# Attention block of a hybrid decoder step: loads two steps ahead, LRU stores not waited for at the block's end, and a turned copy between ScalarE's two exponents

## The reference

```
z = h @ w_in                      # columns: q | k | v | LRU branch | LRU gate
for each of 4 heads, two softmaxes c = 0, 1 over 64-wide halves of q and k:
    s_c = q_c k_c^T / 8 - slope_h * (i - j), causal
    p   = softmax(s_0) - lam * softmax(s_1)
    o   = p @ v                   # 128 wide; RMSNorm, gain g_subln, times (1 - lam_init)
RG-LRU: conv of width 4, gates, linear scan, times gelu(gate branch)
mix = concat(o, lru) @ w_out ;  then the SwiGLU FFN
```

## Time and profile before

| | |
|---|---|
| median of the runs | 3118.41 us |
| the profiled execution, its time | 3117.97 us |
| its span | 3115.9 us |
| PE busy | 2699.2 us (87%) |
| DVE busy | 1691.1 us (54%) |
| ACT busy | 1051.4 us (34%) |
| POOL busy | 912.3 us (29%) |
| chain that ended last | PE 45% of the span, DVE 3%, DMA 2% |

### The profile page before, as it was taken

One profiled execution on the slowest core, in us unless ns is written; L12 is line 12 of the kernel. 1 busy time (PEld: TensorE's weight loads), 2 busy tenths in 40 slices (PEclk: granted clock), 3 DMA queues, 4 the chain that ended last, 5 costly groups with the idle time before them and its releaser, 6 DMA issues.

```text
span 3115.9 us, 42980 instructions
## 1 busy us (share of the span) xinstructions
PE 2699.2 (87%) x16348; PEld 2536.9 (81%) x16348; DVE 1691.1 (54%) x2477; ACT 1051.4 (34%) x1608; POOL 912.3 (29%) x399
## 2 busy tenths in 40 slices
PE   5999998488888656874499999999978999999994
PEld 2999998467777516774499999999978999999993
DVE  2689776567677451667344444444475444444446
ACT  3545553267777503444211111111231111111111
POOL 2566655222332105443122222212241122222212
PEclk8999999699999868987699999999999999999997
DMA  5345433333332255545411111111133111111122
GB/s 217 119 145 190 155 127 128 96 95 82 106 92 65 69 198 194 204 156 176 160 62 41 40 43 58 40 40 61 40 116 90 61 40 40 58 43 40 40 74 55
DMA packets 164737, 300.53 MB, mean 96 GB/s; under 512 B 15402, under 2 KB 131274, under 8 KB 158482
## 3 DMA queue, kind: packets, MB, share of 16 engines
q1 hardware_dynamic: 154850, 283.56, 27.6%
q10 hardware_dynamic: 9776, 15.46, 1.5%
HBM read 252.63 MB, written 46.39 MB: 96 GB/s over the span
## 4 chain that ended last, share of the span: by engine, by line
PE 45%; DVE 3%; DMA 2%; ACT 1%; POOL 0%; issue 0%; DVEq 0%; ACTq 0%; POOLq 0%
PE p_y L1918 15%; PE p_g L1902 15%; PE p_u L1902 15%; DMA p_stage<-h 1%; DVE p_y L2100 1%; DVE p_xin L2112 1%; DVE p_h_lo L2089 1%; ACT p_h_hi L2006 0%; DVE p_rstd L2097 0%; POOL p_stage L1862 0%; DVE p_f_lo L2071 0%; DVE p_y L2083 0%; DMA yT<-p_xin 0%; DMA p_xin<-x 0%; ACT p_stage L2015 0%
## 5 line engine op out<-in xcount | busy, mean ns | idle before, releaser
L2083 DVE TENSOR_TENSOR p_y<-p_y 128x342 f32<-128x342 f32 (+1 forms) x1008 | 483.8, 512 | 730.5 <-PE p_y L1918 730.4
L1902 PE MATMUL p_g<-p_h_hi,p_w_hi 128*128 128x342 f32 (+1 forms) x1056 | 341.7, 324 | 31.5 <-DVE p_h_lo L2089 31.5
L1918 PE MATMUL p_y<-p_f_hi,p_w_hi 128*128 128x342 f32 (+1 forms) x1056 | 344.5, 326 | 26.4 <-DVE p_y L2081 14.2
L329 POOL TENSOR_TENSOR p_w_lo<-p_wraw,p_w_hi 128x1024 fp32r<-128x1024 f32 x100 | 294.5, 2955 | 213.9 <-ACT p_w_hi L390 213.7
L1855 POOL TENSOR_TENSOR p_w_lo<-ffn_wraw,p_w_hi 128x1024 fp32r<-128x1024 f32 x66 | 160.8, 2437 | 639.4 <-ACT p_w_hi L1983 639.4
L1918 PE MATMUL p_y<-p_f_hi,p_w_lo 128*128 128x342 f32 (+1 forms) x1056 | 342.0, 324 | 0.0
L1918 PE MATMUL p_y<-p_f_lo,p_w_hi 128*128 128x342 f32 (+1 forms) x1056 | 341.3, 323 | 0.0
L1902 PE MATMUL p_g<-p_h_lo,p_w_hi 128*128 128x342 f32 (+1 forms) x1056 | 340.3, 322 | 0.0
L1902 PE MATMUL p_g<-p_h_hi,p_w_lo 128*128 128x342 f32 (+1 forms) x1056 | 339.4, 321 | 0.0
L1902 PE MATMUL p_u<-p_h_lo,p_w_hi 128*128 128x342 f32 (+1 forms) x1056 | 338.2, 320 | 0.0
L1902 PE MATMUL p_u<-p_h_hi,p_w_hi 128*128 128x342 f32 (+1 forms) x1056 | 337.4, 319 | 0.0
(11 more groups left out here) (257 smaller groups left out, 5809.5 us busy)
## 6 DMA issues: line engine op xcount, KB each, us to landing
p_wraw<-w_in SPq DMA_DIRECT2D x100, 512.0 KB, 4.7
ffn_wraw<-w_ffn SPq DMA_DIRECT2D x22, 1536.0 KB, 6.5
p_wraw<-w_ffn SPq DMA_DIRECT2D x22, 1536.0 KB, 6.5
p_wraw<-w_out SPq DMA_DIRECT2D x48, 512.0 KB, 7.0
p_ada<-w_ada SPq DMA_DIRECT2D x64, 256.0 KB, 3.2
z<-p_zout SPq DMA_DIRECT2D x48, 206.0 KB, 2.9
p_ada_ring<-w_ada SPq DMA_DIRECT2D x4, 2048.0 KB, 20.9
p_qraw<-z SPq DMA_DIRECT2D x64, 128.0 KB, 3.1
```

Of the source, the lines that this page charges most:

```text
L329: pool.tensor_tensor(w_lo[s][:], wraw[:, s, :], w_hi[s][:].bitcast(F32), ALU.subtract).then_inc(lo_done, 1)
L1902: mm = pe.matmul(bk[par][:, 0:W], a[s][:, KT * half + k, :], b[:, k, c0:c0 + W], start=r == 0, stop=r == 3 * KT - 1)
L1918: mm = pe.matmul(yb[q % YB][:, 0:W], a[s][:, 2 * KT + m, :], b[:, c0:c0 + W], start=r == 0, stop=r == 2)
L2083: dve.tensor_tensor(y[:, m, c0:c0 + W], y[:, m, c0:c0 + W], yb[q % YB][:, 0:W], ALU.add).then_inc(yadd, 1)
```

## The change

- `y_out` outlives `input_projection`: the wait at the block's end goes, and `attention` waits for these stores before the first `read_o` on ScalarE and at step 1 on VectorE; `sample_attention` waits once more at its end.
- Start of attention: q unit 0 is loaded by two DMAs that ScalarE issues; SP starts with k units 0 and 1. ScalarE does the high parts of q 0, k 0, k 1 first, q 1 after. On POOL the low part of q 0 comes before the affine select. The scaling of `gsub` moves into VectorE's step 3, and ScalarE waits for it at step 16.
- Loads of k, q, v are issued in iteration s for step s + 2; `load_ada` keeps its iteration but comes behind them, and is one DMA of 512 KB into one buffer. Output stores keep their iteration.
- In each step ScalarE's order is now exponent 0, `read_v`, turned piece 0, exponent 1, turned piece 1, `read_o`. Before it was exponent 0, exponent 1, `read_v`, pieces 0 and 1, `read_o`.

```diff
@@ input_projection, SP
             sp.dma_start(io["conv_kept"], io["state_conv"][:, 1:3, :]).then_inc(y_out, 16)
-            sp.wait_ge(y_out, 16 * (NG + 3))
             for s in range(RW):
                 sp.wait_ge(z_out[s], 16 * (1 + NG * ZC))
@@ attention, POOL
-            pool.wait_ge(S["ready"], 2)
-            pool.affine_select(out=bias[:], in_=bias[:], compare_op=ALU.is_ge, fill=MASKED, base=SEQ - QB,
...
+            q_low(0)
+            pool.wait_ge(S["ready"], 2)
+            pool.affine_select(out=bias[:], in_=bias[:], compare_op=ALU.is_ge, fill=MASKED, base=SEQ - QB,
@@ attention, SP
             def load_ada(i):
-                for half in range(2):
-                    wait(sp, "rows", i)
-                    sp.dma_start(ada[half][:], io["w_ada"][c, :, 4 * half:4 * half + 4, w0:w0 + AW]
-                                 ).then_inc(ada_in[half], 16)
+                wait(sp, "rows", i)
+                sp.dma_start(ada[:], io["w_ada"][c, :, :, w0:w0 + AW]).then_inc(ada_in, 16)
+            def loads(s):
+                for n in range(1, NQ):
+                    if qstep(n) == s:
+                        load_q(n)
+                for h, u in kpreps.get(s, []):
+                    if s > -1:
+                        load_k(h, u)
+                for h, u in vpreps.get(s, []):
+                    load_v(h, u)
+            for x in kpreps[-1]:
+                load_k(*x)
+            loads(-1)
             sp.dma_start(mods["gsub"][:], io["g_subln"].rearrange("o d -> d o")).then_inc(gs_in, 16)
-            load_q(0)
+            loads(0)
+            load_ada(0)
             for s in range(-1, END):
...
+                loads(s + 2)
+                if adas(s + 1):
                     load_ada(adas(s + 1))
+                for t in oturns.get(s - 1, []):
                     store(t)
@@ attention, ACT
+            for part in (slice(0, DH), slice(DH, P)):
+                act.dma_start(qraw[0][part, :, :], halves(0, slice(UQ * UNITS[0][0], UQ * UNITS[0][0] + UQ))
+                              ).then_inc(q_in[0], 16)
...
+                if s == 0:
+                    act.wait_ge(mods["y_out"], 16 * mods["y_stores"])
...
+            q_high(0)
+            for x in kpreps[-1]:
+                k_high(*x)
             for s in range(-1, END):
+                nt = len(turns(s - 2)) if real(s - 2) else 0
                 if real(s - 1):
                     exps(s - 1, 0)
-                    exps(s - 1, 1)
                 for x in vpreps.get(s, []):
                     read_v(x)
-                nt = len(turns(s - 2)) if real(s - 2) else 0
-                for i in range(min(nt, 2)):
-                    copy_turned(s - 2, i)
+                if nt:
+                    copy_turned(s - 2, 0)
+                if real(s - 1):
+                    exps(s - 1, 1)
+                if nt > 1:
+                    copy_turned(s - 2, 1)
                 if real(s - 3):
                     read_o(s - 3)
@@ attention, DVE, in the loop
+                if s == 1:
+                    dve.wait_ge(mods["y_out"], 16 * mods["y_stores"])
```

More of the change, by code:

```diff
@@ L749, in attention @@
         osb = [buf(f"osb{i}", [P, UQ]) for i in range(2)]
-        ada = [buf(f"ada{i}", [P, 4, AW]) for i in range(2)]
+        ada = buf("ada", [P, KT, AW])
         arow = buf("arow", [P, AW])
@@ L757, in attention @@
         VB = bank("v")
-        k_in, q_in, v_in, ada_in, o_out = ([sem(f"{n}_in{i}") for i in range(2)] for n in ("k", "q", "v", "ada", "osb"))
-        gs_in = sem("gs_in")
+        k_in, q_in, v_in, o_out = ([sem(f"{n}_in{i}") for i in range(2)] for n in ("k", "q", "v", "osb"))
+        gs_in, ada_in = sem("gs_in"), sem("ada_in")
         S = {n: sem(n) for n in (
@@ L788, in vb_free, with halves @@
                     wait(e, "ot_read", ON[x] + 1)
+        def halves(row, ts):
+            return io["z"][row].rearrange("(c p) t -> p c t", c=2)[:, :, ts]
         block = ctx.enter_context(nc.Block())
@@ L828, in scale @@
                                    ).then_inc(S["scaled"], 1)
+            q_low(0)
+            pool.wait_ge(S["ready"], 2)
+            pool.affine_select(out=bias[:], in_=bias[:], compare_op=ALU.is_ge, fill=MASKED, base=SEQ - QB,
+                               pattern=[[-1, SEQ]], channel_multiplier=1).then_inc(S["ready"], 1)
             for s in range(-1, END):
-                for n in range(NQ):
+                for n in range(1, NQ):
                     if qstep(n) == s:
@@ L854, in load_q @@
                 for part in (slice(0, DH), slice(DH, P)):
-                    sp.dma_start(qraw[n % 2][part, :, :],
-                                 io["z"][n // NU].rearrange("(c p) t -> p c t", c=2)[:, :, UQ * u:UQ * (u + 1)]
+                    sp.dma_start(qraw[n % 2][part, :, :], halves(n // NU, slice(UQ * u, UQ * (u + 1)))
                                  ).then_inc(q_in[n % 2], 16)
@@ L1194, in _ @@
                     invert_norm(n)
+                if s == 3:
+                    dve.wait_ge(gs_in, 16)
+                    dve.tensor_scalar(mods["gsub"][:], mods["gsub"][:], 1.0 - LAM_INIT, None, ALU.mult
+                                      ).then_inc(S["gsub"], 1)
                 for h, u in kpreps.get(s, []):
```

39 lines of the change are left out of this document (13 added, 26 removed).

## The result

The changed kernel takes 3144.26 us (median of four runs, 3142.37 to 3149.72) against 3117.35 (3115.30 to 3119.22) for the kernel before in the same runs: ratio 1.0094, 95% interval 1.0081 to 1.0107. The profiled execution took 3143.92 us, its span 3140.6.

A forecast was written before the change was run, and what follows sets the result against it. TensorE was taken to bound the FFN, and attention's end to move the kernel's end. Block's end -3.1, start -1.8, weights +0.5, ScalarE's order +12.4 sum to +8.0 on 3117.97: 3126 us, range 3119 to 3134.

The forecast's parts named there:

- ScalarE's order: Attention term: exponent 1 behind v and piece 0 delays VectorE's reciprocal; +12.4 us, bounds -12.9 and +30.2.
- four long blocks' lateness: Reciprocals after b = 15, 13, 11, 9 in each head: late by 1.6, 1.85, 1.9 and 2.2 us.
- the 3.5 a head that "stays": Lateness reaching TensorE's next turn, less its earlier idle time: 0.5, 1.0, 1.1, 0.9 us; 14.0 in four heads.
- short blocks pass unchanged: Attention's short blocks: ScalarE's new order was claimed to cost nothing there.
- the earlier copy: Piece 0's copy begins one exponent (1.9 us) earlier, but TensorE leaves the step no earlier; no gain counted.
- the clock's term: Clock dip in 755 to 760 us, behind a wait for a copy, goes with that wait: -1.7 us.
- the full price: Rival, attention: every late reciprocal reaches TensorE, 7.55 us a head, 30.2 in all; 3142.1 us; chance 0.10.
- Start: Attention's start: first v load issued earlier despite VectorE and POOL colliding; -1.8 us, between -3.4 and 1.4 lost.
- Modulation weights: Attention: `load_ada` now stands behind a k load that waits for its buffer; +0.5 us, bounds 0 and +3.
- Just in time: Head 0, step 13: modulation weights land at 708.2 us against matmuls at 708.74; other two heads perhaps 0.5 late.
- Block's end: End of input projection: SP's wait for the last store moves into attention, where nothing is late; -3.1 us.
- Two steps ahead: Attention's loads: buffer waits keep them where they were, so no gain; counted as true, without a price.

The follow-up runs named there:

- e1: The changed kernel with ScalarE's old order put back: +2.5 us against the kernel before (-0.3 to 5.3).
- e2: The kernel before with ScalarE's new order as its only edit: +30.5 us against the kernel before (25.9 to 35.2).
- e8: The changed kernel with VectorE's reciprocal behind the first score reduction and the ratio behind the second: +13.1 us against the kernel before.
- e11: e6 with ScalarE's new order only where the exponents' block has b of 8 or more: +26.5 us against the kernel before.
- e10: e6 with ScalarE's new order only where the exponents' block has b under 8: -3.1 us against the kernel before.
- e12: e9 with ScalarE's new order only in even steps, which copy no v: -3.7 us against the kernel before.
- e13: e11 with six needless transposes before TensorE's first turn of even steps with b of 8 or more: +21.2 us against the kernel before.
- e14: The changed kernel with six needless transposes before TensorE's first turn of even steps with b of 8 or more: +28.7 us against the kernel before.
- e6: e1 with the modulation weights' load ahead of the q, k and v loads of its step: -4.1 us against the kernel before.
- e9: e1 with the edits of e6 and e7 together: -1.2 us against the kernel before (-4.4 to 2.2).
- e7: e1 with GpSimd's affine select ahead of q 0's low part again: +1.2 us against the kernel before (-1.2 to 4.1).
- e5: The kernel before with only the wait for the stores moved from the projection's end into attention: +0.3 us against the kernel before.
- e15: e6 with six needless transposes before TensorE's first turn of even steps with b of 8 or more: +1.9 us against the kernel before.

## Why the prediction was wrong

- **Direction and the plain part of the mechanism: right.** ScalarE's order is the cost (e1, e2), and more than half of it goes through the reciprocal at the head of VectorE's list (e8). The four long blocks' lateness came within 0.1 us of the forecast, the 3.5 a head that "stays" came as 3.6 (e11), short blocks pass unchanged (e10), and the earlier copy brought nothing that can be told (e12).
- **The step that failed: the clock's term in "ScalarE's order".** I wrote -1.7, "if the dip of the clock goes with its wait". The wait went, and its dip with it, but 8.5 us of low clock came in e11, 10.2 in the whole change, 17.1 in e2. The new idle of up to 2.5 us (3.0 in e2) before the turn brings dips on as the old wait for a copy had, at more places (e13, e14). The forecast had the row of that dip in hand and applied it to the wait removed but not to the waits added. The term should have been +14 and some +8, about +22, against 27 to 31 timed and 24 to 32 in the stretches. What lies between is in part the next point, in part left open.
- **A part of that step not accounted for:** e11 lies 4.0 us further behind e6 at the reciprocal of step 4 (b = 15 of head 0) than at the store. 1.6 of this is that reciprocal's own lateness, the first long block's, which I had put among the four heads; 0.8 is there when v is first issued, and some 1.7 is low clock in the start. e13, whose code is the same up to there, lies 1.7 behind, so the rest differs from run to run. The stretch of e11 adds up: 22.9 + 4.0 - 1.2 behind step 63 = 25.7.
- **The rival "the full price" came near by luck.** Its 3142.1 stands on all lateness passed on (7.55 a head). Without the clock 3.6 a head arrived, and the clock brought most of the remainder.
- **Start: mis-sized, wrong sign.** -1.8 was forecast for v; it came 0.7 later in the changed kernel and 1.6 in e1. Both of my bounds' causes were true at once: loads behind the stores (q 1.8 to 2.6 us later) and the select's collision, which took both low parts (3.51), not one.
- **Modulation weights: mis-sized.** +0.5 (0 to 3) was forecast, 6.6 measured by e6 against e1 (2.4 by e9 against e7), of which 4.2 is the plain wait. "Just in time" was worked out for head 0; in heads 1 and 2 the wait was up to 2.3.
- **Block's end: right in the profile** (3.0 of 3.1 at the block's start, 2.7 at the end of e5's stretch), not confirmed by the times (e5: +0.3, -2.5 to 2.8).
- **Two steps ahead:** no effect after the start, as counted.

As measured: end and start together -4.1 (e6; forecast -4.9), weights +6.6, order +26.8, in all 29.3, which these three add up to by the way they are formed. In e6's profile only 2.3 of the 4.1 are there at step 4; another 1.0 comes behind step 63 and the rest is within what the times can tell, so that the sum for end and start came near by accident as much as by its steps.

## What to carry to other kernels

On an engine that works its list in order, an instruction put between two parts of a result delays that result until the inserted one's own input is there; ask what waits for the last part, not only what the inserted copy frees. A wait on an engine with slack costs nothing, a wait of the same size in front of the step that bounds is passed on in part (here 3.6 us a head of the 7.4 by which the reciprocals were late), and where it left the matmul engine idle for 2.5 us, a half-speed stretch often came behind it: count dips for waits added, not only for waits removed. A large load that is needed soon goes ahead of small ones that are needed late.

## What the runs showed of the hardware

- Low clock came in portions: between equal places of different kernels it was 0.0, 1.7, 3.4 or 5.1 us (head 2 of e6, e5, e13 and e11), and one portion cost 1.6 us of time (head 1, from the reciprocal of step 18 to that of 34: 110.07 us in e9, 111.64 in e6). Kernels with the same code in a head can differ by one portion.
- VectorE's scaling of the bias took 2.28 us beside GpSimd's low part of q 1 (changed kernel) and 1.21 alone (kernel before).
- VectorE's two low parts beside two GpSimd instructions that followed each other at once took 3.51 us (changed kernel), beside one 1.81, and alone 1.29.
- Six transposes of 128 x 128 in a row took TensorE 0.82 us at full clock (e13, e14, e15).
